# First mixer: four inverses in step, blocks transposed on VectorE, and a work list for each engine

## The reference, cut to what matters

```
def rwkv7_step(S, inp):                          # one token, 8 heads of 64
    r_t, w_t, k_t, v_t, kk_t, a_t = inp
    sa = einsum("bhvk,bhk->bhv", S, -kk_t)
    S = S * w_t + sa (x) (kk_t * a_t) + v_t (x) k_t
    y = einsum("bhvk,bhk->bhv", S, r_t)
...                                              # then a norm of y per head, a bonus, a gate
def rglru_mix(xb, gb, ...):                      # the other half of the width
    xc = causal convolution of xb over 4 tokens
    r, i_g = sigmoid(xc @ gate_a), sigmoid(xc @ gate_x)
    h = scan of h*a + sqrt(1 - a*a) * i_g * xc, with a = exp(-8 * r * softplus(-lam))
    return h * gelu(gb)
return concatenate([ya, yb]) @ w_out
```

## Time and profile before

| | us |
|---|---|
| median of 3 runs | 3524.36 (3523.35 to 3532.81) |
| the profiled execution | 3532.7 |
| its span | 3530.6 |
| inverses and recurrence of the first mixer | 535.06 to 740.57 |
| PE, DVE, ACT busy over the span | 96%, 56%, 38% |

### The profile page before, as it was taken

The page is one execution under the profiler, slowest core; times in us unless marked ns, Lnnn a source line. Parts: engine busy times, 40 slices in busy tenths (PEclk is TensorE's granted clock), DMA queues, the critical chain, the costliest instruction groups (busy, mean ns, idle before and its releaser), DMA issues.

```text
span 3530.6 us, 48359 instructions
## 1 busy us (share of the span) xinstructions
PE 3395.6 (96%) x20836; PEld 2734.4 (77%) x20836; DVE 1990.6 (56%) x2864; ACT 1337.6 (38%) x2006; POOL 4.1 (0%) x18
## 2 busy tenths in 40 slices
PE   8999986899999999999999999999999999999998
PEld 7888865778888788887588888766888887578887
DVE  5554676357554754353655434566766455866644
ACT  4332454133322433233633322254544233644433
POOL 0000000000000000000000000000000000000000
PEclk9999996699999999999999999999999999999999
DMA  5444430014444342222013223210232231013221
GB/s 191 143 143 143 136 109 21 3 66 143 145 147 144 131 140 99 96 92 84 1 66 108 96 98 126 94 54 25 84 107 96 100 139 60 31 60 108 96 96 60
DMA packets 93093, 342.49 MB, mean 97 GB/s; under 512 B 10320, under 2 KB 10960, under 8 KB 92368
## 3 DMA queue, kind: packets, MB, share of 16 engines
q1 hardware_dynamic: 92880, 339.40, 28.4%
HBM read 337.26 MB, written 2.10 MB: 96 GB/s over the span
## 4 chain that ended last, share of the span: by engine, by line
PE 85%; DVE 8%; ACT 5%; issue 1%; DMA 0%; SPq 0%; DVEq 0%; ACTq 0%
PE ps L780 20%; PE ps L781 20%; PE ps L782 20%; PE ps L816 3%; PE ps L812 3%; PE ps L813 3%; DVE SPL L2048 1%; PE ps L851 1%; PE ps L850 1%; PE ps L849 1%; ACT WK L1942 1%; PE ps L1207 1%; PE ps L835 1%; PE ps L836 1%; PE ps L837 1%
## 5 line engine op out<-in xcount | busy, mean ns | idle before, releaser
L2048 DVE TENSOR_TENSOR SPL<-RAW,SPH 128x1024 fp32r<-128x1024 f32 x522 | 635.9, 1224 | 963.4 <-ACT SPH L1452 963.3
L780 PE MATMUL ps<-HH,SPH 128*128 128x512 f32 x2332 | 921.1, 395 | 9.9 <-DVE SCR L2138 4.6
L1452 ACT ACTIVATE SPH<-RAW 128x1024 fp32r<-128x1024 f32 x522 | 547.9, 1056 | 998.5 <-PE ps L782 879.3
L781 PE MATMUL ps<-HL,SPH 128*128 128x512 f32 x2332 | 910.2, 390 | 0.0
L782 PE MATMUL ps<-HH,SPL 128*128 128x512 f32 x2332 | 910.1, 390 | 0.0
L780 PEld LDWEIGHTS ps<-HH,SPH 128*128 128x128 f32 x2332 | 438.9, 188 | 113.8 <-issue 10.7
L781 PEld LDWEIGHTS ps<-HL,SPH 128*128 128x128 f32 x2332 | 438.7, 188 | 93.5 <-issue 4.1
L782 PEld LDWEIGHTS ps<-HH,SPL 128*128 128x128 f32 x2332 | 438.8, 188 | 91.6
L780 PE MATMUL ps<-AH,SPH 128*128 128x512 f32 x1008 | 394.2, 391 | 0.0
L782 PE MATMUL ps<-AH,SPL 128*128 128x512 f32 x1008 | 392.8, 390 | 0.0
L781 PE MATMUL ps<-AL,SPH 128*128 128x512 f32 x924 | 360.0, 390 | 0.0
(11 more groups left out here) (499 smaller groups left out, 4169.5 us busy)
## 6 DMA issues: line engine op xcount, KB each, us to landing
RAW<-in_ws SPq DMA_DIRECT2D x522, 512.0 KB, 3.3
RAW<-in_wa SPq DMA_DIRECT2D x96, 512.0 KB, 3.3
WK<-in_sm SPq DMA_DIRECT2D x2, 2784.0 KB, 9.9
WK<-in_cst SPq DMA_DIRECT2D x2, 1664.0 KB, 6.7
X<-in_x SPq DMA_DIRECT2D x8, 256.0 KB, 8.0
out<-X SPq DMA_DIRECT2D x8, 256.0 KB, 2.0
WK<-in_sm SPq DMA_DIRECT2D x1, 768.0 KB, 4.8
PCT<-in_pc SPq DMA_DIRECT2D x1, 349.0 KB, 3.0
```

The costliest lines, as they stand in the source:

```text
L780: e.matmul(out, wh, rhs[0], start=start, stop=False)
L781: e.matmul(out, wh, rhs[1], start=False, stop=False)
L1452: e.activation(SPH[:, q:q + 1024], RAW[:, r:r + 1024], ACT.Copy).then_inc(hi_ready.did(("hi", n)))
L2048: e.tensor_tensor(SPL[:, q:q + 1024], RAW[:, r:r + 1024], SPH[:, q:q + 1024].bitcast(F32), ALU.subtract).then_inc(lo_ready.did(("lo", n)))
```

## The change

Each engine gets a list of its own. The four chunks are inverted in step, levels 1 to 4 make only the inverse on TensorE, and VectorE transposes it by blocks of 32 (`wt`). `MT` and `RK` share a stationary operand and become one product `MK` of 256 columns. The products of chunk c+1 stand between the steps of chunk c; `sp` stands between the parts of `yp`. Buffers for the additional chunks lie in SPH and SPL, so the last four chunks of weights (22 to 25 of this stage) are not halved in the projection part but in the lists, after `yp` of chunk 2. The tiny matmuls for the modulation move from chunks 14 to chunks 0 modulo 16, and the addition after them (`mods`) by one piece.

```
+MIX0_TENSOR = [("ld", 0), ("ld", 1), ("lt", 0), ("nm", 0, 1), ("nm", 1, 1), ("lt", 1), ("nm", 2, 1), ("nm", 3, 1),
+               ("gates", 0), *all_chunks("dd", 1), ("lt", 2), *all_chunks("nm", 2), ("gates", 1), *all_chunks("dd", 2),
+               ("lt", 3), *all_chunks("nm", 3), ("vt",), *all_chunks("dd", 3), *all_chunks("nm", 4),
+               *all_chunks("dd", 4), ("MK", 0), *all_chunks("nm", 5), ("RB", 0), *all_chunks("dd", 5), ("tr", 0),
+               *all_chunks("nm", 6), *all_chunks("dd", 6),
+               ("r0p", 0), ("MK", 1), ("sap", 0), ("RB", 1), ("spyp", 0), ("tr", 1), ("gates", 2),
+               ("r0p", 1), ("fmean", 0), ("MK", 2), ("sap", 1), ("fvar", 0), ("RB", 2), ("fg", 0), ("spyp", 1), ("tr", 2),
+               ("gates", 3),
+               ("r0p", 2), ("fmean", 1), ("MK", 3), ("sap", 2), ("fvar", 1), ("RB", 3), ("fg", 1), ("spyp", 2), ("tr", 3),
+               ("r0p", 3), ("fmean", 2), ("sap", 3), ("fvar", 2), ("fg", 2), ("spyp", 3),
+               ("fmean", 3), ("fvar", 3), ("fg", 3)]
...
+MIX0_VECTOR = [("conv", 0), ("w0", 0), ("w0", 1), ("nmc", 0, 1), ("nmc", 1, 1), ("conv", 1), ("ltm", 0), ("nmc", 2, 1),
...
+               ("fy", 1), ("iu", 3), ("MKm", 3), ("RBm", 3), ("fn", 1), ("state", 2), ("gm2", 3), ("hy", 2), ("ylo", 1),
+               ("fy", 2), ("ml", 2), ("halve", 23), ("fn", 2), ("hy", 3), ("halve", 25), ("ylo", 2), ("ml", 3),
+               ("fy", 3), ("fn", 3), ("ylo", 3)]
...
+MIX0_SCALAR = [("xc", 0), ("xc", 1), ("ldc", 0), ("ldc", 1), ("gelu",), ("tanh", 0), ("tanh", 1), ("p2", 0), ("vt",),
+               ("p2", 1), ("sq", 0), ("sq", 1), *all_chunks("nmc5"), *all_chunks("w5"), ("mh", 0), *all_chunks("nmc6"),
...
+               ("r0", 2), ("tanh", 3), ("fq", 1), ("sa", 2), ("frs", 1, True), ("p2", 3), ("yc", 2), ("tr", 3), ("sq", 2),
+               ("yhi", 1),
+               ("r0", 3), ("fq", 2), ("sa", 3), ("mh", 2), ("sq", 3), ("halve", 23), ("frs", 2, True), ("yc", 3),
+               ("halve", 25), ("yhi", 2), ("mh", 3), ("fq", 3), ("frs", 3, False), ("yhi", 3)]
...
-                if c % 16 == 14 and c < 2 * N_ADA:
-                    b = c // 16
+                if c % 16 == 0 and 0 < c <= 2 * N_ADA:
+                    b = c // 16 - 1
...
-                                    for r in range(0, 128, 32):
-                                        rs = slice(r, r + 32)
-                                        mm = e.matmul(b[rs, ut], n[rs, us], Wc[rs, ut], start=True, stop=True,
-                                                      skip_group_check=True)
...
-                    halve_to(ahead_of(s, i))
+                    halve_to(min(ahead_of(s, i), BASE[s] + 21))
...
+                def transposed(c, lv):
+                    Wc = inv["W"][c]
+                    w.wait_ge(("w", c, lv), *([("dd", c, lv)] if lv else []))
+                    e.transpose(Wc[:, 256:512], Wc[:, 0:256]).then_inc(dve_done.did(("wt", c, lv)))
...
+                    elif what == "w":
+                        Wc = inv["W"][c]
+                        w.wait_ge(("dd", c, lv), ("w", c, lv - 1), ("wt", c, lv - 1))
+                        e.tensor_tensor(Wc[:, 0:256], Wc[:, 0:256], ps["dd", c, lv][:, 0:256], ALU.add).then_inc(
+                            dve_done.did(("w", c, lv)))
```

More of the change, by code:

```diff
@@ L192, with all_chunks @@
 BONUS_SUMS_AT, BONUS_AT = {12: 0, 15: 1, 18: 2, 21: 3}, {13: 0, 16: 1, 19: 2}
[L194 to L210, removed]
+def all_chunks(what, *x):
+    return [(what, c, *x) for c in range(4)]
@@ L587, in norm @@
[L587 to L600, removed]
-                if i == 1:
+            for what, *x in MIX0_TENSOR:
+                if what == "gates":
+                    ps.plan(("ga", *x), ("gta", *x))
+                    ps.plan(("gx", *x), ("gtx", *x))
+                elif what == "ld":
+                    for hf in range(2):
+                        ps.plan(("ld", *x, hf), ("ldc", *x, hf))
+                elif what == "lt":
+                    for hf in range(2):
+                        ps.plan(("lt", *x, hf), ("ltm", *x, hf))
+                elif what == "nm":
+                    ps.plan(("nm", *x), ("nmc", *x))
+                elif what == "dd":
+                    ps.plan(("dd", *x), ("w", *x))
+                elif what == "vt":
@@ new lines, in chunk @@
+                def chunk(what, c):
+                    cs = slice(128 * c, 128 * c + 128)
+                    KT_, BT_ = rwkv["KT"][c], rwkv["BT"][c]
+                    if what == "MK":
+                        w.wait_ge(("prep_dd",))
+                        for half in range(2):
+                            w.wait_ge(*ps.before("MK", c, 0, half), *ps.before("MK", c, 1, half))
+                            for j in (2 * half, 2 * half + 1):
+                                for hf in range(2):
+                                    p0, o = slice(64 * hf, 64 * hf + 64), 256 * (j % 2)
+                                    mm = e.matmul(
+                                        ps["MK", c, hf, half][:, o:o + 256].rearrange("p (k t) -> p k t", k=2),
+                                        wk(K[j])[p0, cs], WKu[p0, j:j + 19:18, cs], start=True, stop=True)
+                            mm.then_inc(pe_done.did(("MK", c, half)))
+                    elif what == "RB":
+                        products("RB", c, AA, R)
+                    elif what == "tr":
@@ L1148, in mix0 @@
[L1148 to L1151, removed]
-                    if i == 1:
+                for what, *x in MIX0_TENSOR:
+                    if what == "ld":
+                        blocks32(*x)
+                    elif what == "lt":
+                        products("lt", *x, AA, KK)
+                    elif what == "nm":
+                        off_diagonal(*x)
+                    elif what == "dd":
+                        joins(*x)
+                    elif what == "gates":
+                        gates(*x)
+                    elif what == "vt":
@@ L2264, in lru @@
                             former = done
-                    elif part == 1:
+                    elif what == "iu":
                         w.wait_ge(("gtx", j), ("conv", j))
@@ L2268, in lru @@
                             dve_done.did(("iu", j)))
-                    elif part == 2:
+                    elif what == "gm2":
                         w.wait_ge(("a2", j))
@@ L2272, in lru @@
                             dve_done.did(("gm2", j)))
-                    elif part == 3:
+                    elif what == "hy":
                         w.wait_ge(("sqrt", j), ("iu", j))
```

672 lines of the change are left out of this document (330 added, 342 removed), and 4 rows, old and new, of tables (MIX0_SCALAR, MIX0_VECTOR).

## The result

The changed kernel took 3510.23 us (median of four runs, 3506.6 to 3512.4) against 3528.44 for the kernel before in the same measurement: ratio 0.995, interval 0.9935 to 0.9964. In a second measurement, of six and eleven runs, it took 3507.33 against 3529.96: 0.9938, interval 0.9924 to 0.9952. So it is faster, by 18 to 23 us. The forecast was 3493, in a range of 3466 to 3514; the time lies in the range, 17 us above the forecast.

A forecast was written before the change was run, and what follows sets the result against it. In the rewritten inverses TensorE was taken to be bound by instruction arrival, 128 matmuls and 128 loads per 3.88 us. Output projection 27.4 us earlier plus 3.9 for modulation, 31.3 off the median 3524.4, gave 3493, range 3466 to 3514.

The forecast's parts named there:

- Head: Start of the rewritten mixer stretch: TensorE's wait for VectorE's `prep_dd` after the last projection goes, gain 4.7 us.
- Inverses up to level 5: First mixer's inverses: 1344 of 4928 records removed in the stage, the rest arriving at 30.3 ns each; level 5 ends at 612.9.
- Level 6 and the chunks: Level 6 takes 16 us at clock 0.50; recurrence of chunk 0 begins at 628.9, chunk 3 at 682.3.
- Tail: From chunk 3 on, VectorE's and ScalarE's queues make 28.9 us; output projection begins at 711.2, plus 2 us for restart.
- Rival B: The tail's queue is shorter than drawn, 17 to 20 us instead of 28.9: 3481 to 3484; chance 0.15.
- Modulation: Making the sums of `ada` two chunks later removes TensorE's waits in three places: -3.9 us, at worst 0.
- The base: Profiled execution 3532.7 lies 8.3 above the median of the runs shown, 3524.4; the 31.3 were subtracted from that median.
- Rival A: Clock rises early: level 6 and chunk 0 run at 1.00, 7.4 + 7 us go, restart costs nothing: 3477; chance 0.18.
- Rival C: Arrival isn't the rule (records worth 10 to 14.5 ns), or VectorE and ScalarE stop each other: 3508 to 3513; chance 0.20.

The follow-up runs named there:

- a_tail: The changed kernel with only VectorE's and ScalarE's lists reordered around chunk 3 of the first mixer's recurrence: 3500.33 us, ratio 0.9917 to the kernel before.
- a_mod14: The changed kernel with only the modulation put back to chunks 14, 30, ... (`mods` back by one piece with it): 3498.01 us, ratio 0.9913.
- b_again: The kernel before itself, unchanged, measured once more: 3525.47 us, ratio 0.9999.
- a_dense: The changed kernel with 16 unused matmuls of 128x512 added, one ahead of each group of `nm` and `dd` at levels 4 and 5: 3501.48 us, ratio 0.9918.
- best3: The changed kernel with modulation back at chunks 14, 30, ..., the reordered tail and 16 unused 128x512 matmuls ahead of levels 4 and 5: 3487.86 us, ratio 0.9879.
- a_dense2: The changed kernel with 16 unused matmuls of 128x512 added ahead of levels 2 and 3: 3514.06 us, ratio 0.996.
- a_more: The changed kernel with the 1024 records of the transposed half of `dd` put back at levels 1 to 4, results unused: 3541.59 us, ratio 1.0028.
- a_wide: The changed kernel with the 32x32 matmuls of levels 1 to 4 streaming their columns twice, same number of records: 3507.72 us, ratio 0.9937.
- best2: The changed kernel with the modulation back at chunks 14, 30, ... and the reordered tail, without long matmuls: 3495.22 us, ratio 0.99.
- a_again: The changed kernel itself, unchanged, measured once more: 3507.33 us, ratio 0.9938.
- b_mod0: The kernel before with only the modulation moved to chunks 16, 32, ..., first mixer untouched: 3533.11 us, ratio 1.0004.
- b_mod0_again: The kernel before with only the modulation moved to chunks 16, 32, ..., measured a second time: 3532.87 us, ratio 1.0012.

## Why the prediction was off, step by step

The sum was made against the profiled execution: 3532.7 - 31.3 = 3501.4, and then laid on the median. The profiled executions of the changed kernel took 3506.6 and 3503.6, and the median of the result is 3510.2. The steps:

- *Head*, 4.7: right. In the timeline of after the level-0 products begin 1.02 us behind the last projection; VectorE is no longer waited for.

```profile
530.16 1.02 PE L978 MATMUL ps<-SCR,CST 128*128 128x512 f32 x2
531.18 2.15 PE L1018 MATMUL ps<-WK 64*32 64x32 f32 x228
535.47 0.35 PE L1018 MATMUL ps<-WK 64*32 64x32 f32 x28 [2.14 <-issue]
...
589.10 0.26 PE L1034 MATMUL ps<-SCR,ACC 32*32 32x32 f32 x1 [1.65 <-issue]
593.07 0.26 PE L1034 MATMUL ps<-INV 32*32 32x32 f32 x1 [1.92 <-issue]
```

- *Inverses up to level 5*: right. The first gap ends at 535.47 (forecast 535.5), gaps follow at 3.5 to 4.0 us for 128 records or twice that for 256, level 5 ends at 612.8 (612.9). The average from 535.47 to 599.98 is 29.7 ns a record (30.3 forecast), and the waits for other engines came to 4.0 us (2 forecast), so two small errors cancel here. The transposes of 128x256, taken as 0.45 from rows of 128x1024 and 128x512, are 0.42 to 0.44, and no wait of PE names them. Groups of VectorE from 530 to 713:

```profile
L2323 DVE STREAM_TRANSPOSE SCR<-SCR 128x256 f32<-128x256 f32 x8 | 3.5, 437 | 0.0
...
L2323 DVE STREAM_TRANSPOSE INV<-INV 128x256 f32<-128x256 f32 x8 | 3.1, 419 | 0.0
```

- *Level 6 and the chunks*: right in size. Chunk 0 begins at 628.2 (628.9) and chunk 3 at 681.9 (682.3). The chain of after that ended last, which answers to the earlier trace rows:

```profile
614.74 6.70 PE ps L1042 x61
621.75 6.46 PE ps L1065 x61
628.21 1.90 PE ps L1098 x16
630.11 3.60 PE ps L1106 x16
...
702.33 2.27 DVE SPL L2068 x2
704.60 0.60 DVE AH L2413
705.20 0.60 DVE HL L2305
705.80 0.61 DVE SCR L2397
706.44 0.64 ACT SCR L1739
707.12 2.08 PE ps L1179 x2
709.19 1.51 PE ps L1185 x8
710.71 0.24 PE ps L801
```

- *Tail*: right, and the same rows show it. The halving (L2068) ends at 704.6, `ylo`, `ml` and `fy` follow, then the square, `fvar`, `fg`; the projection begins at 710.71 (forecast 711.2 and 2 us of restart). The restart at the lower clock came in another place: TensorE had been idle 8.6 us, the granted clock was 0.51 from 700 to 710, and `fvar` and `fg` took 2.08 and 1.51 where those of chunk 0 took 0.91 and 1.09 at the full clock, 1.6 us more; the projection itself ran at 0.23 a matmul from its start. Rival B, the shorter queue, did not come for this order, and a_tail shows that reordering it is worth 7 us.
- ***Modulation*, -3.9: this step failed.** The three waits at L762 did go, but the step was costed as a wait taken away on VectorE and the place of the accumulator in the ring of banks was not followed. Moved, it costs 8.4 to 9.8 us within FFN2 (6.6 of them the wait at tile 6), and putting it back alone made the changed kernel 9.3 us faster, part of which may be the clock at level 6 (a_mod14). The bounds I gave it, -3.9 to 0, excluded a loss; the plan of eight banks in the code, six tiles and two, would have shown it.
- *The base: this failed too.* The 31.3 were read from the slower course of the kernel before and subtracted from 3524.4, a median of three, two of them near the faster one. The profile of b_again took the faster course: from its span the changed kernel's is only 19.6 us shorter (3524.5 to 3504.9), near the 18.2 of the medians. And in the measurement that gave the result the kernel before had 3528.4, not 3524.4 (in the later groups 3525 to 3533). The profiled execution was held to be the outlier, but it was one of two courses.

An estimate of the 17.2 us from these numbers: 4.1 are the median of the kernel before (3528.4 in place of 3524.4). The other 13.1 are the gain, 18.2 in place of 31.3. Between the two profiles that the forecast compared the spans differ by 25.7, which is 5.6 short: 8.1 were lost behind the start of the output projection (4.2 given back in place of 3.9 gained, the modulation) and 2.5 won before it. The slower course accounts for another 6.1 (25.7 less 19.6), and 1.4 stay open. That the time still fell into the range is no merit of these two steps.

Rival A deserves its own line. The clock stayed at 0.50 through level 6, as forecast, so its time did not come; but my reason against it was unsound. The row from 682 to 698 that I took as proof that unbroken work doesn't raise the clock is one of two courses of the same kernel (b_again). It still stands: TensorE was busy all 16.00 us at 0.50, and why it stayed there is open. Just ahead of level 6, from 591 to 602, TensorE was busy 6.0 of 11 us in after, with gaps of "issue" between; with the long matmuls in those gaps it was busy all 11.00, and the full clock came (a_dense, likewise best3, not a_dense2). The Trainium skill, "TensorE: Matmul & The Clock Gate", section "What's actually happening", says that activity releases the throttle. At level 6 a_dense bears this out: 1.00 where after had 0.50.

Rival C fell in its first part (a_more, a_wide: records are worth their arrival, not their execution). Its second, engines that stop each other, appears only as 2.8 us at L1034 and 1.2 at L1004.

## What to carry to other kernels

When TensorE stands for "issue" between many tiny matmuls, count records, not columns: removing 1024 of them gave 27 us, doubling what each streamed gave nothing, and another engine may do their work even if it is slow. When a step is moved, follow its buffer as well as its wait: count who holds every bank at the new place, at the start of every stage. Before a row is used as proof of what the clock does, look at a second execution, and do not subtract what one execution shows from a median that others made. Gaps in which TensorE only waits for instructions can hold long matmuls, and just ahead of dense work these brought the clock back and paid; two levels earlier the same matmuls cost more than the gaps held.

## What the hardware showed that I had not expected

- Two executions of one kernel differ by 6 us, most of it in one stretch and with the clock: 0.50 and 1.00 from 682 to 698, both 16.00 us busy, with 137 and 230 records. A second kernel with the same mixer showed the same two courses.
- Added work made the kernel faster: 16 matmuls of 128x512 gave 5.8 us beside the changed kernel and 7.4 on top of best2; moved two levels earlier they cost 6.7. Level 6 ran at 1.00 with them and at 0.50 to 0.66 without.
- A record in levels 1 to 4 cost 30.3 ns when 1024 were added (a_more against after, by the traces), whatever it streamed, and 680 and 673 of them passed in 20 us at a granted 1.00 and 0.67.
- A wait of 6.6 us at the start of a stage cost 8.4 to 9.8 in all: behind it the clock was low for seven matmuls, and at the end of the stage, 330 us later, it dipped to 0.83 over 10 us in the five profiles with the wait that were read there (after, a_again, a_tail, b_mod0, b_mod0_again), and was 1.00 in before and a_mod14. Why is open.
